# Scores of the first memory attention from stacks of high parts and remainders, and one value-projection piece moved to the first step

## The reference, cut to what matters

```python
q = rms_norm_2(qm.reshape(B, S, MEM_HEADS, MEM_HDIM), qn_g)   # 4 heads of 64
k = rms_norm_2(kv[..., :MEM_W].reshape(B, M, MEM_HEADS, MEM_HDIM), kn_g)
s = jnp.einsum('bshd,bmhd->bhsm', q, k).astype(jnp.float32) * (MEM_HDIM ** -0.5)
p = jax.nn.softmax(s, axis=-1)
o = jnp.einsum('bhsm,bmhd->bshd', p.astype(v.dtype), v)
```

## Time and profile before

| what | value |
|---|---|
| median of 3 runs | 1678.35 us (1676.62 to 1679.75) |
| profiled execution | 1679.82 us, span 1678.0 us |
| mean granted TensorE clock | 0.998 |
| PE busy | 1660.4 us, 99% of the span |
| PEld, DVE, ACT, POOL busy | 81%, 53%, 47%, 42% |
| POOL low parts (L644) | 257 of 2.4 us |
| ACT splits (L1306) | 257 of 1.06 us |

### The profile page before, as it was taken

How to read it: one execution, slowest core, us unless ns; L and a number is a source line. 1 busy time by engine, 2 the same in 40 slices (tenths; PEclk the granted TensorE clock), 3 DMA queues, 4 the chain that set the end, 5 groups by cost and what they waited for, 6 DMA issues and landing times.

```text
span 1678.0 us, 24465 instructions
## 1 busy us (share of the span) xinstructions
PE 1660.4 (99%) x8381; PEld 1361.3 (81%) x8381; DVE 896.8 (53%) x1718; ACT 781.1 (47%) x1213; POOL 704.5 (42%) x372
## 2 busy tenths in 40 slices
PE   9999999999999999999999999999999999999999
PEld 6788678888987899888888888888767888888887
DVE  6799877558426487646555531152554555555100
ACT  6323566337454545445545432345564455445222
POOL 4344212444634576344444444444202444444445
PEclk9999999999999999999999999999999999999999
DMA  6233211433422210233333333322201323333333
GB/s 223 76 113 107 76 39 62 153 100 104 137 89 88 76 39 26 64 89 100 100 92 96 99 101 101 112 95 88 64 1 51 89 100 100 96 91 100 101 113 113
DMA packets 44381, 153.56 MB, mean 92 GB/s; under 512 B 4976, under 2 KB 5104, under 8 KB 44272
## 3 DMA queue, kind: packets, MB, share of 16 engines
q1 hardware_dynamic: 41184, 145.10, 27.9%
q10 hardware_dynamic: 3120, 7.43, 1.3%
HBM read 150.15 MB, written 2.10 MB: 91 GB/s over the span
## 4 chain that ended last, share of the span: by engine, by line
PE 88%; DVE 4%; issue 4%; POOL 2%; ACT 1%; DMA 0%; POOLq 0%; SPq 0%; ACTq 0%; DVEq 0%
PE DB L1179 9%; PE DB L1178 9%; PE DB L1177 9%; PE DB L744 8%; PE DB L746 8%; PE DB L745 8%; PE DB L1196 5%; PE DB L1198 5%; PE DB L1197 5%; PE SC L873 3%; PE SC L1059 2%; PE DB L893 2%; PE DB L797 2%; POOL WL L644 1%; PE DB L799 1%
## 5 line engine op out<-in xcount | busy, mean ns | idle before, releaser
L644 POOL TENSOR_TENSOR WL<-RAW,WH 128x1024 fp32r<-128x1024 f32 x257 | 618.5, 2407 | 924.8 <-ACT WH L1306 922.1
L1306 ACT ACTIVATE WH<-RAW 128x1024 fp32r<-128x1024 f32 x257 | 272.4, 1060 | 597.5 <-PE DB L746 177.8
L1177 PE MATMUL DB<-XH,WH 128*128 128x512 f32 x640 | 249.0, 389 | 0.0
L1178 PE MATMUL DB<-XL,WH 128*128 128x512 f32 x640 | 249.0, 389 | 0.0
L1179 PE MATMUL DB<-XH,WL 128*128 128x512 f32 x640 | 249.0, 389 | 0.0
L744 PE MATMUL DB<-XH,WH 128*128 128x512 f32 x568 | 228.8, 403 | 3.8 <-POOL WL L644 2.3
L746 PE MATMUL DB<-XH,WL 128*128 128x512 f32 x568 | 221.7, 390 | 0.0
L745 PE MATMUL DB<-XL,WH 128*128 128x512 f32 x568 | 221.4, 390 | 0.0
L1178 PEld LDWEIGHTS DB<-XL,WH 128*128 128x128 f32 x640 | 120.1, 188 | 25.1
L1177 PEld LDWEIGHTS DB<-XH,WH 128*128 128x128 f32 x640 | 120.1, 188 | 24.9
L1179 PEld LDWEIGHTS DB<-XH,WL 128*128 128x128 f32 x640 | 120.1, 188 | 24.9
(11 more groups left out here) (517 smaller groups left out, 2947.9 us busy)
## 6 DMA issues: line engine op xcount, KB each, us to landing
RAW<-in_stream_dram SPq DMA_DIRECT2D x267, 512.0 KB, 3.5
TP<-in_toep_dram ACTq DMA_DIRECT2D x4, 512.0 KB, 3.6
X<-in_xt_dram ACTq DMA_DIRECT2D x1, 2048.0 KB, 13.8
out_dram<-X SPq DMA_DIRECT2D x8, 256.0 KB, 4.3
X<-in_xt_dram ACTq DMA_DIRECT2D x4, 256.0 KB, 6.4
X<-in_xt_dram SPq DMA_DIRECT2D x4, 256.0 KB, 6.1
MRAW<-in_memt_dram ACTq DMA_DIRECT2D x2, 512.0 KB, 4.8
CONST<-in_consts_dram SPq DMA_DIRECT2D x1, 448.0 KB, 8.8
```

Source lines behind the costliest of these rows:

```text
L644: nc.gpsimd.tensor_tensor(WL[:, s, :], RAW[:, j, :], WH[:, s, :].bitcast(F32), ALU.subtract).then_inc(lo_done, 1)
L1177: mm(o, WH[:, s, c], xh(k), start=(k == 0), stop=False)
L1178: mm(o, WH[:, s, c], xl(k), start=False, stop=False)
L1306: A(WH[:, n % SPLIT, :], RAW[:, n % RING, :], ACT.Copy).then_inc(hi_done, 1)
```

## The change

The scores of the first memory attention are made from stacks of 128 rows. QMS0 holds for each head the fp32r high part of the queries in the head's own 64 rows and their remainder in the other 64; MKH0 holds the high part of the keys in both halves of the rows, MKL0 their remainder in both halves. A score is then two fp32r matmuls, QMS0 by MKH0 and QMS0 by MKL0. ScalarE makes the high parts behind the sigmoids of hf1 to hf4 (two copies of 64 x 1024, four of 64 x 512); VectorE makes the remainders behind the scaling of hf4 and of hf5 (eight subtractions of 64 x 512). TensorE waits for four counts of each remainder ahead of the attention. The number of value pieces in turn 0 goes from none to one, in turn 6 from two to one.

```diff
+        QMS0 = at("QMS0", [P, 4, TOK], A0 + 56, F32R)
+        MKH0 = at("MKH0", [P, 4, MEM], A0 + 64, F32R)
+        MKL0 = at("MKL0", [P, 4, MEM], A0 + 12, F32R)
@@ steps_m
-                        yield dict(rq=RQM[:, c:c + 1], both=RQM[:, c - e:c - e + 2], qk=[(q[r, p, P * i:P * i + P], MKT[l][r, p, :])], w=MEM,
+                        qk = [(q[r, p, P * i:P * i + P], MKT[l][r, p, :])]
+                        if l == 0:
+                            qk = [(QMS0[:, h, P * i:P * i + P], k[:, h, :]) for k in (MKH0, MKL0)]
+                        yield dict(rq=RQM[:, c:c + 1], both=RQM[:, c - e:c - e + 2], qk=qk, w=MEM,
@@ TensorE
-            pe.wait_ge(hs_done, HEADS["qm01"][0] + 1)
+            pe.wait_ge(qm0_low, 4)
+            pe.wait_ge(mk0_low, 4)
             attention(segments["m0"], [], itertools.chain(*(token_tiles(f"hv{k}", xh, xl, 384) for k in range(2))),
-                      lambda k: (0, 2, 2, 2, 2, 2, 2, 1, 1, 1, 1)[k])
+                      lambda k: (1, 2, 2, 2, 2, 2, 1, 1, 1, 1, 1)[k])
@@ ScalarE, in the loop over hf{k}
+                if k in (1, 2):
+                    A(QMS0[HALF[k - 1], k - 1:4:2, :], QM[HALF[k - 1], :, :], ACT.Copy).then_inc(qm0_high, 1)
+                if k in (3, 4):
+                    act.wait_ge(hs_done, HEADS["mk01"][0] + 1)
+                    for half in (HALF[k - 3], HALF[4 - k]):
+                        A(MKH0[half, k - 3:4:2, :], MKT[0][HALF[k - 3], :, :], ACT.Copy).then_inc(mk0_high, 1)
@@ VectorE
-            for k in (4, 5):
-                root_scaled(f"hf{k}")
+            root_scaled("hf4")
+            for e, r in enumerate(HALF):
+                dve.wait_ge(qm0_high, e + 1)
+                for p in range(2):
+                    V.tensor_tensor(QMS0[HALF[1 - e], 2 * p + e, :], QM[r, p, :], QMS0[r, 2 * p + e, :].bitcast(F32),
+                                    ALU.subtract).then_inc(qm0_low, 1)
+            root_scaled("hf5")
+            for e, r in enumerate(HALF):
+                dve.wait_ge(mk0_high, 2 * e + 2)
+                for half in HALF:
+                    V.tensor_tensor(MKL0[half, e:4:2, :], MKT[0][r, :, :], MKH0[r, e:4:2, :].bitcast(F32),
+                                    ALU.subtract).then_inc(mk0_low, 1)
```

More of the change, by code:

```diff
@@ L456, in build @@
         o_high = sem("o_high")
+        mk0_high = sem("mk0_high")
+        mk0_low = sem("mk0_low")
+        qm0_high = sem("qm0_high")
+        qm0_low = sem("qm0_low")
         sums_done = sem("sums_done")
```

## The result

The changed kernel takes 1690.11 us (median of 4 runs, 1689.07 to 1690.19), the kernel before in the same series 1679.05 us. The ratio is 1.0065, 95% interval 1.0054 to 1.0077: 11.1 us slower. The forecast was 1686.8 us, slower by 8.4, with a range from 1683.5 to 1690.3.

A forecast was written before the change was run, and what follows sets the result against it. It took TensorE's matmul work to bound the kernel, 88% of the chain that ended last. The turns' +6.9 and the clock's +1.5, copies at nothing, gave +8.4 us: 1678.35 becomes 1686.8 us, range 1683.5 to 1690.3.

The forecast's parts named there:

- The step on which it stood: Attention turns 3 to 5: slab ready 5.86 us after the transposes, wanted after 3.05, a new 2.96 us wait each turn.
- The sum by turns: Attention, TensorE: turns 0 to 2 +0.5, turns 3 to 5 +8.1, turn 6 -2.4, turn 7 +0.7; sum +6.9 us.
- the clock: TensorE's clock may fall behind each of three new waits, 1.5 us a fall; one fall likeliest: +1.5, bounds 0 and +4.5.
- 0.36 us a pair: Attention scores: two fp32r matmuls over 128 rows instead of fp32 over 64 save this; 2.9 us for eight pairs if nothing binds.
- the clock falls behind two or three waits: Rival: the clock falls behind two or three of the attention's new waits, +9.9 to +11.4, 1688.3 to 1689.8 us; chance 0.27.
- Part 3: ScalarE's copies and VectorE's remainder subtractions ahead of the attention: costed at 0, bounds -0.7 and +0.7 us.
- the other bound: Query pieces: a VectorE chain shifted in time may leave GpSimd's 3.12 us low part alone, a gain of 0.7 us.
- the result of its lock: VectorE's subtractions collide with GpSimd's under an exclusive port lock: 0.7 us late, the sum then +7.6.
- No slab is late: Rival: every low part in the attention is there 3.05 us after the transposes; -3.2, 1675.2 us; chance 0.07.
- Half absorbed: Rival: half of the lateness is absorbed, the split ready about 1.5 us earlier; 1680 to 1681.7 us; chance 0.07.

The follow-up runs named there:

- the piece from turn 1: The full change, but turn 0's value piece is taken from turn 1 instead of turn 6 (pieces 1,1,2,2,2,2,2,1,1,1,1): 1675.47 us, ratio 0.9974.
- the scores alone: The full change with the old numbers of pieces, so without the moved piece: 1676.98 us, ratio 0.9987.
- the stacks unused: High parts and remainders made and waited for, but scores still fp32 from queries and keys over 64 rows, pieces as before: 1678.47 us, ratio 0.9996.
- the piece alone: The kernel before with only the piece moved from turn 6 to turn 0, scores still fp32 over 64 rows: 1690.28 us, ratio 1.0058.
- the filled waits: The full change plus 14 unused 384-column matmuls between the two pieces of turns 3, 4 and 5: 1685.25 us, ratio 1.0040.
- the split a turn ahead: The full change with its pieces, but ScalarE splits each value slab one turn earlier and empties the first value job's banks before: 1677.87 us, ratio 0.9990.

## Why the prediction was right, point by point

**Direction and mechanism.** The step on which it stood, a slab ready 5.86 us after the transposes and wanted after 3.05, held: the wait appears at the named place, three times, and goes both when the first use is put back (the piece from turn 1) and when the split is put ahead. That is shown, from both sides. The waits were somewhat shorter than forecast, 2.65 us against 2.96 and 1.0 against some 1.3.

**The sum by turns.** Transposes of turn 2: forecast 0.5 later, measured 0.2 earlier (539.91 against 540.09), since the stage ahead ended half a microsecond earlier (527.77 against 528.25) and the third slab, which the sum had just too late, was not waited for. Turns 3 to 5: forecast 8.1 and 1.5 for the clock, measured 569.23 - 539.91 = 29.32 against 18.46, 10.9 more. A turn without a fall took 8.70 us (548.61 - 539.91), forecast 8.85. Turn 6: 3.77 (573.00 - 569.23), forecast 3.73. Turn 7: 5.01, forecast 5.12. Together 8.9 in the profile where the forecast had 8.4. That the two are so close is in part luck: without the falls the attention is 5.8 us longer in the first profile and 5.6 in the second where the sum had 6.9, and the falls cost 3.1 and 4.2 where it had 1.5. The two errors go against each other.

**From the profile to the median.** The forecast median is 3.3 us too low. Of these, 0.5 is the sum above, 0.9 the third fall, 0.4 the time behind the attention (1099.4 against 1099.0), and 1.5 is the step that turned the profiled execution into a median: the kernel before was profiled in an execution 1.5 us above its median, and I took the same off for the kernel after. But the second profile of the changed kernel, 1690.06 us, is at its median, and the first, 1689.07, is below it. That subtraction had no reason in the mechanism, and it is the largest single part of the miss.

**The scores.** 0.36 us a pair was nearly right: with the scores alone, turn 3 takes 5.79 us (538.83 to 544.62) against 6.11 before (540.09 to 546.20), and the next three are 0.32 to 0.33 us shorter too. The attention ends 2.8 us earlier, of which 0.7 is the stage ahead (the stacks unused) and 2.1 the scores. That it is worth nothing in a waiting turn was in the sum (the turn was counted from the arrival of the slab) but not said; the piece alone shows it.

**The term that was too small: the clock.** "I give each a chance of some 0.4, and the likeliest count is one" failed. Two fell in the first profile and three in the second, and the runs point to three as the usual count. One fall cost about what was computed, 1.5 us: 1.56 in the first profile (3.85 against 2.29 for a piece) and 1.37 to 1.45 in the second. So the term is 3.1 to 4.2 us instead of 1.5. With three falls the rival "the clock falls behind two or three waits" had 1689.8 us; its mechanism is what came, and its number is so close only because the parts above cancel. That the falls are caused by the waits was only argued from the earlier trace rows then; the filled waits show it, 0 falls of 3. The rule that I set beside it, the Trainium skill (TensorE: Matmul & The Clock Gate, "HAM oscillation — how this bites in real kernels"), repeated waits making the clock fall again and again, is borne out: in the second profile the clock falls behind each of the three, and so it does with the piece alone. The page tells it of longer waits, for a DMA; here it fell behind waits of 2.3 us too.

**Part 3.** Costed at nothing with bounds of 0.7 us either way. The group of the trace after, VectorE's subtractions for the queries (those for the keys, L2227, look the same):

```profile
L2221 DVE TENSOR_TENSOR QMS<-QM,QMS 64x512 fp32r<-64x512 f32 x4 | 4.8, 1234 | 0.1
```

Four take 4.8 us. The mean of 1.2 hides two kinds: by the view of the tile QMS (shortest, median and longest in ns) three of a group take 0.69 and one 2.9:

```profile
L2221 DVE TENSOR_TENSOR QMS<-QM,QMS x4: 681/686/2885, 490.2 to 494.3; 64x512 fp32r<-64x512 f32 x4
```

GpSimd's low part runs beside them, from 490.56 to 493.10. This is the collision that the prediction named, once in a job; it came out at 4.8 us and not at 3.0 + 2.4. VectorE waited 4.74 for TensorE there, so hf5 is scaled 0.14 us late (495.00 instead of 494.86) and VectorE's scans behind it shift. It is the other bound that came in sign: TensorE's wait ahead of hq2 is 0.42 us and not 1.15, because the low part for it took 2.39 us instead of 3.12. The two engines in the trace before, VectorE's scan, and in the one after, GpSimd's low part and the scan:

```profile
503.07 1.23 DVE L2210 TENSOR_TENSOR_SCAN HB<-RESET,HB 128x512 f32<-128x512 f32 x1
```

```profile
503.58 2.39 POOL L654 TENSOR_TENSOR WL<-RAW,WH 128x1024 fp32r<-128x1024 f32 x1 [5.04 <-ACT WH L1317]
503.60 3.46 DVE L2237 TENSOR_TENSOR_SCAN HB<-RESET,HB 128x512 f32<-128x512 f32 x1
```

Before, the scan starts first, 0.28 us ahead of the low part (503.35): the scan takes 1.23 us and the low part 3.12. After, the low part starts first by 0.02 us: it takes 2.39 and the scan 3.46. All eight traces with the copies and remainders have the second order and the two without them (before, and the piece alone) have the first. So the gain, which the prediction had as its lower bound, rests on a shift of VectorE by 0.3 us. The Trainium skill (SBUF — State Buffer, "Who interferes with whom") made me name 0.7 late as the result of its lock; the lock agrees with these rows, but the price that I worked out from it did not come: 0.14 late, and a gain behind it.

**The rivals.** "No slab is late" had its condition made in the split a turn ahead; it gives 1677.9 us and not 1675.2. Its attention ends 1.8 us earlier than before and not 3.2: TensorE waits 0.76 us for the bank in turn 4, and VectorE's output holds turn 7 by 1.30 us instead of 0.27. "Half absorbed" did not occur: nothing behind the attention gave anything back (1099.0 and 1099.4 us).

## What to carry to other kernels

When work is moved between steps of a loop to fill a hole, count for every buffer that it uses the moment of first use against the moment at which the producer's own order lets it be ready; a shift by half a buffer early in a loop is a shift of every later first use. The same hole can be filled by the neighbour's work: taking the piece from turn 1 gives 0.26% where taking it from turn 6 costs 0.65%. A wait of TensorE of 2.3 to 2.7 us should be priced with the clock that it may lose behind it, here 1.4 to 1.6 us on top of each fall. And a forecast that starts from a profiled execution should say how far that execution lies from the median, and why the same distance should hold after the change.

## What the runs showed of the hardware that I had not expected

The clock fell behind eight of nine waits of 2.3 to 2.7 us: two of three in the first profile of the changed kernel, three of three in the second, three of three with the piece alone, where the waits were 2.3 us. Each time TensorE had done wide matmuls up to the wait. The ninth wait, turn 3 of the first profile, was 2.65 us long and left the clock at 1.00, so the length of the wait alone does not decide; what does is open. The clock did not fall behind the wait of 1.0 us in turn 7, nor in the three places where 14 wide matmuls left a wait of 0.24 us.

The time behind the attention is not the same from run to run: 1096.3 us in two profiles (the piece from turn 1, and the filled waits) and 1097.8 to 1101.0 in the others. The two have a granted clock of 1.00 between 1160 and 1240 us, the others 0.94 to 0.98. The two go together: 1.00 less the clock, times these 80 us, is 1.6, 3.2 and 4.8 us at 0.98, 0.96 and 0.94, and the time behind the attention is 1.5, 2.7 to 3.2 and 4.7 us above the 1096.3. This is a spread of up to 4.7 us from falls of the clock that no edit here touched, and the reason why differences of one microsecond were read from the start of hg0.
